# A gated projection stage split into three passes: seven block products for u and z, a DRAM round trip, and an output projection of two tiles per PSUM sum

## The reference

```python
def odd_mixer(h, sg_norm_g, w_in, w_spatial, b_spatial, w_out):
    p = jnp.einsum('bsd,de->bse', h, w_in)
    u, v, z = _split(p, ODD_SIZES)              # 2048 columns each
    u = jax.nn.gelu(u)
    v = rmsnorm(jax.nn.gelu(v), sg_norm_g)
    vg = v.reshape(B, nc, SG_CHUNK, SG_GROUPS, SG_GROUP_DIM)
    wm = w_spatial * causal
    vs = jnp.einsum('gts,bcsgd->bctgd', wm, vg) + b_spatial.T[None, None, :, :, None]
    y = u * vs.reshape(B, S, SG_WIDTH) * jax.nn.silu(z)
    return jnp.einsum('bse,ed->bsd', y, w_out)
```

## Time and profile before

| | us |
|---|---|
| median of 3 runs | 2878.29 (2877.9 to 2878.43) |
| the profiled execution: its own time | 2879.76 |
| its span, first to last instruction | 2878.0 |
| values stage and before | up to 2278.4 |
| gating stage, tiles 0 to 15 without the last pass | 2278.4 to 2828.2 |
| last pass, norm and store | 2828.2 to 2878.0 |

### The profile page before, as it was taken

The page is one execution under the profiler, slowest core; times in us unless marked ns, Lnnn a source line. Parts: engine busy times, 40 slices in busy tenths (PEclk is TensorE's granted clock), DMA queues, the critical chain, the costliest instruction groups (busy, mean ns, idle before and its releaser), DMA issues.

```text
span 2878.0 us, 38876 instructions
## 1 busy us (share of the span) xinstructions
PE 2753.0 (96%) x14218; PEld 2204.1 (77%) x14218; DVE 1497.4 (52%) x2252; ACT 889.8 (31%) x1500; POOL 1352.2 (47%) x792
## 2 busy tenths in 40 slices
PE   6999999999988999999998999999989999999997
PEld 2588888888776777777776888888688878888885
DVE  6665445455465555566556464546430045555555
ACT  3642322322253333334332323222431321111112
POOL 0587676776553322222221443433254465555564
PEclk9999999999999999999998999999999999999998
DMA  9211111111121110001001111211232311111123
GB/s 386 91 52 51 46 56 51 51 54 47 44 82 40 36 37 22 29 30 36 29 30 37 45 51 41 54 53 50 85 128 75 115 59 59 58 58 59 58 66 125
DMA packets 62904, 185.40 MB, mean 64 GB/s; under 512 B 17108, under 2 KB 23380, under 8 KB 60648
## 3 DMA queue, kind: packets, MB, share of 16 engines
q1 hardware_dynamic: 42016, 152.68, 15.9%
q10 hardware_dynamic: 20808, 31.61, 3.2%
HBM read 163.22 MB, written 21.05 MB: 64 GB/s over the span
## 4 chain that ended last, share of the span: by engine, by line
PE 85%; DVE 6%; issue 3%; ACT 3%; DMA 1%; POOL 1%; DVEq 0%; ACTq 0%; SPq 0%; POOLq 0%
PE ps L886 26%; PE ps L888 25%; PE ps L887 25%; PE ps L1297 2%; DVE acc L2570 1%; PE ps L954 1%; PE ps L1308 1%; DMA resid<-x_t 1%; PE ps L1060 1%; PE ps L1027 1%; PE ps L1654 1%; ACT sg_z L2346 1%; PE ps L1345 0%; PE ps L987 0%; DVE da_al L2787 0%
## 5 line engine op out<-in xcount | busy, mean ns | idle before, releaser
L637 POOL TENSOR_TENSOR slab_hi<-slab_raw,zero 128x1024 fp32r<-128x1024 f32 x165 | 328.7, 1992 | 1142.6 <-PE ps L888 997.0
L886 PE MATMUL ps<-h_hi,slab_hi 128*128 128x512 f32 x1936 | 771.1, 398 | 11.5 <-POOL h_lo L655 7.0
L887 PE MATMUL ps<-h_lo,slab_hi 128*128 128x512 f32 x1936 | 759.0, 392 | 0.0
L888 PE MATMUL ps<-h_hi,slab_lo 128*128 128x512 f32 x1936 | 758.2, 392 | 0.0
L886 PEld LDWEIGHTS ps<-h_hi,slab_hi 128*128 128x128 f32 x1936 | 365.8, 189 | 99.8 <-issue 15.4
L888 PEld LDWEIGHTS ps<-h_hi,slab_lo 128*128 128x128 f32 x1936 | 365.6, 189 | 79.2
L887 PEld LDWEIGHTS ps<-h_lo,slab_hi 128*128 128x128 f32 x1936 | 366.2, 189 | 72.4
L641 POOL TENSOR_TENSOR slab_lo<-slab_raw,slab_hi 128x1024 fp32r<-128x1024 f32 x165 | 413.0, 2503 | 14.6 <-DVE mean L2670 1.7
L2570 DVE TENSOR_TENSOR acc<-ps,acc 128x512 f32<-128x512 f32 x352 | 228.3, 686 | 24.7 <-PE ps L888 23.5
L2596 DVE SCALAR_TENSOR_TENSOR resid<-ps,mod,resid 128x512 f32<-128x512 f32 x320 | 224.6, 751 | 0.2
L702 POOL TENSOR_TENSOR slab_lo<-slab_raw,slab_hi 128x512 fp32r<-128x512 f32 x124 | 162.3, 1316 | 44.3 <-ACT slab_hi L1847 43.6
(11 more groups left out here) (371 smaller groups left out, 4977.3 us busy)
## 6 DMA issues: line engine op xcount, KB each, us to landing
slab_raw<-w_in SPq DMA_DIRECT2D x168, 512.0 KB, 3.6
mod_big<-mod_w SPq DMA_DIRECT2D x12, 2048.0 KB, 11.2
slab_raw<-w_c SPq DMA_DIRECT2D x43, 512.0 KB, 3.6
res_scr<-resid ACTq DMA_DIRECT2D x4, 2048.0 KB, 7.2
resid<-res_scr ACTq DMA_DIRECT2D x2, 4096.0 KB, 13.0
gv_scr<-sg_t ACTq DMA_DIRECT2D x4, 2048.0 KB, 7.0
slab_raw<-gv_scr SPq DMA_DIRECT2D x16, 512.0 KB, 3.4
resid<-x_t SPq DMA_DIRECT2D x2, 2048.0 KB, 16.3
```

What stands on the lines that cost most here:

```text
L637: pool.tensor_tensor(hi, raw[slot][:], zeros, ALU.add).then_inc(hi_done.sem, 1)
L886: pe.matmul(dst, w_h, r_h, start=first, stop=False, skip_group_check=True)
L887: pe.matmul(dst, w_h, r_l, start=False, stop=False, skip_group_check=True)
L888: return pe.matmul(dst, w_l, r_h, start=False, stop=last, skip_group_check=True)
```

## The change

The gating stage becomes three passes.

1. For each of the 16 tiles, u and z are made together as seven block products of 12 matmuls (84 instead of 96). ACT and DVE turn them into gelu(u) times silu(z) (`gu_` tiles), and the product is stored to DRAM (`uz_scr`). The input sums that the scheme needs are made by DVE during the values stage.
2. The spatial products no longer stand between u and z. Tiles 0 and 1 are done inside the last turn of pass 1, and the others inside pass 3.
3. The output projection takes two tiles at a time (`sg_pair`), both summed in PSUM before DVE adds 16 pieces per pair instead of 16 per tile. The stored `uz_scr` tile is read back and multiplied with the spatial result. The last two tiles keep their own last pass.

The scaled spatial weights are now made by ACT in eight pieces per group (one DVE instruction before). The high parts of the weight slabs move from POOL to ACT. POOL no longer clears `acc`. The last pass itself keeps its order.

```diff
+GATE_ORDER = (A11, S1, A12, S3, S4, S2, A22)
+GATE_LAST_ORDER = (A11, S3, S1, A12, S4, S2, A22)
+LAST_GATE = SG_TILES - 1
+SG_PAIRS = SG_TILES // 2 - 1
...
+            def load_gate(f, s):
+                sp.wait_ge(u_lo.sem, u_lo.at(f - 1, GATE_ORDER.index((A12, A22)[s])))
+                load_ring(f, s, w_in, 2 * f + (IN_SG + s), in_load[s])
+            def store_gate(f):
+                sp.wait_ge(u_mul.sem, u_mul.at(f))
+                sp.dma_start(uz_scr[bass.ds(f, 1)].rearrange("a p t -> p (a t)"), uz_out[:]).then_inc(uz_st.sem, 16)
...
+            def load_uz(d):
+                if d < 2:
+                    sp.wait_ge(u_mm.sem, u_mm.at(LAST_GATE, gate_product(LAST_GATE, S3)))
+                else:
+                    sp.wait_ge(e_yl.sem, e_yl.at(d - 2))
+                sp.wait_ge(uz_st.sem, uz_st.at(d))
+                sp.dma_start(uz[d % 2][:], uz_scr[d]).then_inc(uz_ld[d % 2].sem, 16)
...
+            def gate_sums(f):
+                for load in in_load:
+                    pool.wait_ge(load.sem, load.at(T_SG // 2 + f))
+                a21 = gate_source(S3)
+                pool.tensor_tensor(gu_s1[:], a21, gate_source(A22), ALU.add).then_inc(u_sum.sem, 1)
+                pool.wait_ge(u_sum.sem, u_sum.at(f, 0))
+                pool.tensor_tensor(a21, gate_source(A11), a21, ALU.subtract).then_inc(u_sum.sem, 1)
+                pool.tensor_tensor(gu_s2[:], gu_s1[:], gate_source(A11), ALU.subtract).then_inc(u_sum.sem, 1)
+                pool.wait_ge(u_sum.sem, u_sum.at(f, 2))
+                pool.tensor_tensor(gu_s4[:], gate_source(A12), gu_s2[:], ALU.subtract).then_inc(u_sum.sem, 1)
+            def gate_low(f, j):
+                pool.wait_ge(u_hi.sem, u_hi.at(f, GATE_ORDER.index(j)))
+                low, high = (gate_ring(tile, last, j).rearrange("p k f -> p (k f)") for tile, last in ((all_lo, u_lo6), (all_hi, u_hi6)))
+                pool.tensor_tensor(low, gate_source(j), high.bitcast(F32), ALU.subtract).then_inc(u_lo.sem, 1)
...
+            gate_sums(LAST_GATE)
+            for j in GATE_ORDER[:4]:
+                gate_low(LAST_GATE, j)
+            spatial_low(0)
+            for j in GATE_ORDER[4:]:
+                gate_low(LAST_GATE, j)
+            values_low(1)
+            for n in range(4):
+                slab_low(0, n)
+            y_low(0)
+            spatial_low(1)
+            y_low(1)
+            values_low(2)
...
+                last = q == SG_PAIRS - 1
+                if q > 0:
+                    slab_low(q, 2)
+                    slab_low(q, 3)
+                values_low(2 * q + 3)
+                y_low(2 * q + 2)
+                if last:
+                    split_c(TC_SG + SG_TILES)
+                else:
+                    slab_low(q + 1, 0)
+                    slab_low(q + 1, 1)
+                    values_low(2 * q + 4)
+                    spatial_low(q + 2)
+                y_low(2 * q + 3)
...
-            def sg_tile(d, e, g, first):
-                pe.wait_ge(e_u.sem, e_u.at(d - 1))
-                if first and e == 0:
-                    pe.wait_ge(v_g.sem, v_g.at(NC * (SV_SETS - 1) + 5))
-                project(T_SG + 2 * d, 0)
...
+            def gate_block(f, j):
+                pe.wait_ge(u_lo.sem, u_lo.at(f, GATE_ORDER.index(j)))
+                w_h, w_l = gate_ring(all_hi, u_hi6, j), gate_ring(all_lo, u_lo6, j)
+                r_h, r_l = GATE_INPUT[j]
+                for k in range(KT // 2):
+                    mm = three(FFN_BANK[j], w_h[:, k, :], w_l[:, k, :], r_h[:, k, :], r_l[:, k, :],
+                               k == 0 and j in FFN_OPENS, k == KT // 2 - 1)
+                mm.then_inc(u_mm.sem, 1)
...
+            def gate_ready(f, j):
+                if j == A11:
+                    pe.wait_ge(u_gate.sem, u_gate.at(f - 1, 0))
+                elif j == S1:
+                    pe.wait_ge(u_c.sem, u_c.at(f - 1, 0))
+                elif j == A12:
+                    pe.wait_ge(u_pc.sem, u_pc.at(f, 0))
+                elif j == S3:
+                    pe.wait_ge(u_c.sem, u_c.at(f - 1, 2))
+                elif j == S4:
+                    pe.wait_ge(u_pc.sem, u_pc.at(f, 1))
+                elif j == S2:
+                    pe.wait_ge(u_u.sem, u_u.at(f - 1))
+                else:
+                    pe.wait_ge(u_y.sem, u_y.at(f))
...
-            def sg_turn_out(g, e):
-                sg_tile(2 * g + e, e, g, False)
-                pe.wait_ge(e_v.sem, e_v.at(2 * g + e))
-                sg_out(2 * g + (e - 1), 1 - e, TC_SG + 4 * g + 2 * e)
...
+            gate_ready(0, A12)
+            gate_block(0, A12)
+            turned_ready(10)
+            gate_block(0, S3)
+            gate_ready(0, S4)
+            gate_block(0, S4)
+            pe.wait_ge(v_g.sem, v_g.at(NC * SV_SETS - 1))
+            turned_ready(11)
+            gate_block(0, S2)
+            gate_ready(0, A22)
+            turned_ready(15)
...
+            with pe.Fori(1, LAST_GATE) as f:
+                for j in GATE_ORDER:
+                    gate_ready(f, j)
+                    gate_block(f, j)
+            for j in GATE_LAST_ORDER:
+                if j == S3:
+                    sg_spatial(0)
+                if j == S4:
+                    sg_spatial(1)
+                gate_ready(LAST_GATE, j)
+                gate_block(LAST_GATE, j)
...
+            def sg_pair(q):
+                slabs = [(s, *sy[q % 2][s]) for s in range(2)]
+                for t in range(2 * KT):
+                    d, e = divmod(t, 2)
+                    if d % 4 == 0 and e == 0:
+                        pe.wait_ge(o_lo.sem, o_lo.at(q, d // 2 + 1))
+                    if t == 0:
+                        pe.wait_ge(e_yl.sem, e_yl.at(2 * q + 1))
+                    bank_free(q, t)
+                    for n, (s, r_h, r_l) in enumerate(slabs):
+                        mm = three(BANK[4 + t % 4], whi[s][:, d, :], wlo[s][:, d, :], r_h[:, half_of(e)], r_l[:, half_of(e)],
+                                   n == 0, n == 1)
+                    mm.then_inc(o_mm.sem, 1)
+                    if t in (1, KT - 1):
+                        sg_spatial(2 * q + (2 if t == 1 else 3))
+            for q in range(SG_PAIRS):
+                sg_pair(q)
...
+            def gate_high(f, j):
+                if j in RING_SUM_GATE:
+                    act.wait_ge(u_sum.sem, u_sum.at(f, RING_SUM_GATE[j]))
+                else:
+                    s = 1 if j == A22 else 0
+                    act.wait_ge(in_load[s].sem, in_load[s].at(T_SG // 2 + f))
+                act.activation(gate_ring(all_hi, u_hi6, j).rearrange("p k f -> p (k f)"), gate_source(j), ACT.Copy).then_inc(u_hi.sem, 1)
+            def gate_next(f, j):
+                act.wait_ge(u_mm.sem, u_mm.at(f - 1, gate_product(f - 1, j)))
+                gate_high(f, j)
...
+            def spatial_weights(g):
...
+                for c in range(NC):
+                    act.activation(wr[:, c, :], wsp[:, g, :], ACT.Identity, scale=stat[:, NC + c:NC + c + 1],
+                                   bias=zero[:, 0:1]).then_inc(w_s.sem, 1)
                 act.wait_ge(w_s.sem, w_s.at(g))
-                act.wait_ge(in_mm.sem, in_mm.at(T_SG + 4 * g - 1))
                 act.activation(wr_hi[:], wr[:], ACT.Copy).then_inc(w_h.sem, 1)
...
-            def sg_tile(d, e):
-                act.wait_ge(in_mm.sem, in_mm.at(T_SG + 2 * d))
-                act.wait_ge(e_y.sem, e_y.at(d - 1))
-                act.activation(sg_u[:], PS[0], ACT.Gelu_apprx_tanh).then_inc(e_u.sem, 1)
-                act.wait_ge(in_mm.sem, in_mm.at(T_SG + 2 * d + 1))
-                act.activation(sg_z[:], PS[1], ACT.Silu).then_inc(e_z.sem, 1)
-                act.wait_ge(e_y.sem, e_y.at(d))
-                act.activation(sy_hi[e][:], sg_v[:], ACT.Copy).then_inc(e_yh.sem, 1)
...
+            def gate_turn(f, first=False):
+                gate_copy_first(f, first)
+                gate_next(f + 1, A11)
+                gate_next(f + 1, S1)
+                gate_copy_fifth(f, first)
+                gelu_first(f, first)
+                for j in (A12, S3, S4, S2):
+                    gate_next(f + 1, j)
+                gelu_second(f)
+                gate_next(f + 1, A22)
+                silus(f)
+            for k in range(KT // 2):
+                act.wait_ge(tin_sum.sem, tin_sum.at(k))
+                act.wait_ge(c_mm.sem, c_mm.at(TC_SG - 1))
+                act.activation(h_hi[:, k, HALF:T], g4_raw[:, k, :], ACT.Copy).then_inc(tin_hi.sem, 1)
...
+            for j in (S4, S2):
+                gate_high(0, j)
+            act.wait_ge(v_st[1].sem, v_st[1].at(SV_SETS // 2 - 1))
+            gate_high(0, A22)
+            gate_turn(0, first=True)
...
+            with act.Fori(1, LAST_GATE) as f:
+                gate_turn(f)
+            spatial_weights(0)
...
+            def gate_sums(f):
+                dve.wait_ge(u_mm.sem, u_mm.at(f, gate_product(f, S2)))
```

(15 more changed lines are left out.)

455 lines of the change are left out of this document (338 added, 117 removed).

## The result

The changed kernel takes **2861.9 us** (median of 5 runs, 2859.7 to 2866.2) against 2878.3: ratio 0.9945, 95% interval 0.993 to 0.9959, so it is 16.4 us faster where 35.0 were forecast. The profiled execution is its fastest, 2859.7 us with a span of 2858.0.

A forecast was written before the change was run, and what follows sets the result against it. PE, by its number of matmuls, was taken as the bound. Work 493.0 plus waits 6, 13 and 5 gives 517.0 us against 549.8; with the last pass −35.0, so 2843.3 us, range 2832 to 2861.

The forecast's parts named there:

- Block products: Gating stage: seven products take 19.22 us per turn, 16 turns 307.5 against 351.4 before, −43.9 us.
- Spatial and output products: Gating stage: same pace, 28.6 and 156.9 us; the 6.4 and 6.5 us of old waits go.
- Turns 1 to 14: Gate turns: slab, ACT and POOL chains all fit under PE's 19.22 us, so 0 us extra.
- POOL's circle: POOL's repeating work per gate turn: load wait 3.8, four sums, seven low parts, 17.9 us, spare 1.3.
- The rival of a longer gate turn: Gate turns: hand-overs use up their spare and add 1.2 us a turn, 18 in all: 2861 us; 14%.
- POOL held off by DVE: Gate turns: DVE's passes over SBUF tiles slow POOL's pieces, 3.9 us per turn over PE, about 2901 us; 4%.
- Turn 0: First gate turn: PE waits 3.3 us after S1 and 2.3 before S4, a clock drop hidden; 6 us taken.
- Turn 15: Last gate turn: waits of 6.8, 1.6 and 2.4 us plus 2.1 for half clock, together 13 us.
- Pairs 0 to 5: Output pairs of 26.0 us: POOL's y part comes late, at least 26.8; 0.8 each, six times, 5 us.
- the pairs wait more: Output pairs: 2 us beyond the forecast wait in each of seven, 2857 us; 9%.
- Last pass: Final pass: its two waits of 1.1 us go, −2.2 us.

The follow-up runs named there:

- experiment 7: Changed kernel with the values' high part ahead of the spatial weights (2845.3 us), but output projections taking one tile at a time in PSUM: 2863.9 us.
- experiment 10: The kernel with ACT's copies of A11 and S1 moved earlier (2865.2 us), plus a DVE wait starting products after POOL's next A22 low part: 2858.7 us.
- experiment 5: Changed kernel with ACT's copy of A11 earlier in turn 0 and its copy of S1 ahead of the next turn's S1 part: 2865.2 us.

## Why the prediction was off

The direction and the mechanism of the gain were right, the size was not: 16.4 of 35.0 us came, and 2861.9 lies 0.9 above the range. Point by point, by the numbers of the prediction:

1. *Block products*: right. 19.27 us where 19.22 stood.
2. *Spatial and output products*: right. A pair's work is 26.1 us, the pace unchanged; experiment 7 shows that DVE's adds would cost 18.6 us more.
3. *Turns 1 to 14*: 0 extra, right in the sum. Its margin was not. I wrote that POOL's circle has a spare of 1.3 us; it is 0.9 (18.3 in experiment 10), and only while DVE's products fall in POOL's wait for the slabs. In experiment 5 they don't, the slabs come later too, and the circle is 19.9. The rival of a longer gate turn (14%) didn't happen. The rival "POOL held off by DVE", at 4%, named a part of this mechanism; it came not in the changed kernel but in the mended one, at 0.65 us a turn where the rival had 3.9.
4. *Turn 0*: right, 25.3 us for 25.2. The first wait is 2.98 for 3.3. Of the second nothing is seen, and that was forecast: half clock cost the products behind the first wait 3.0 us, and ACT's copy of S1 was done at 2293.85, 16.55 us after the values for 16.6, 0.4 before S4 began.
5. *Turn 15*: 2.8 short. Its three waits were sized well, 7.4, 2.6 and 1.4 us from matmul to matmul, less 0.23 each that is the pace, are 10.7 where 6.8 + 1.6 + 2.4 = 10.8 stood. The clock was not: 38.6 less 22.9 of work and 10.7 leaves 4.9 for 2.1. I costed one stretch of half clock, as long as the one in the earlier trace rows. After 7 us of waiting the spatial product and two blocks behind it, 7.3 us of work, took 10.7, from 2582.33 until ACT could copy S1 (row below). The other 1.6 us are a second stretch, behind the wait of 2.20.

```profile
2593.01 0.60 ACT L2654 ACTIVATE gu_p<-ps 128x512 f32<-128x512 f32 x1 [12.14 <-PE ps L1048]
```

6. *Pairs 0 to 5*: **the step that failed**, 5 us forecast, 18.4 more than 6 × 26.0 measured. I had the right chain (y stands last on POOL) and took 0.8 a pair for its overhang. It is 2.1: in pair 0 ACT starts its weights at 15.5 us and not at 14.9, its chain takes 5.2 and not 4.7, as a 128-column piece is 0.40 (3.20 for eight) and not 0.33, and POOL's first part 2.98 and not 2.4, as DVE's product falls beside it. Three small terms, all rounded the kind way, on a chain whose slack was already below zero. And the consequence I left out altogether: behind such a wait the clock may halve, 1.6 us each, here at three of six heads. Waits 12.4 and clock 4.7 make 17.1 of the 17.5 above 6 × 26.15. The rival "the pairs wait more" (9%) is what happened.
7. *Last pass*: right, 2858.0 − 2811.38 = 46.6 us where 49.8 were before, so −3.2 for −2.2. The values ended 1.1 us sooner too (2277.3 for 2278.4), which no item had. Both were luck on my side: the stage is 17.1 us over, the span 15.0.

The last 3.6 us are not the trace's: I took the median 0.3 above the profiled span, and the profiled execution was the fastest of five. Part of the runs' spread lies ahead of the stage; what it comes from stays open.

Of the drain of 1380 ns that the Trainium skill ("ScalarE: Activation LUTs", "What ACT_TABLE_LOAD costs") adds to a table load the trace after shows nothing: the load starts 0.03 us after the activation before it has ended, and the activation behind it 1.29 us after the load, so 1.28 was the right term.

```profile
2572.59 0.63 ACT L2546 ACTIVATE gu_hi<-slab_raw 128x512 fp32r<-128x512 f32 x1 [0.72 <-PE ps L1048]
2573.25 1.28 ACT L2671 ACT_TABLE_LOAD   x1
2574.54 0.63 ACT L2671 ACTIVATE gu_u<-gu_u 128x512 f32<-128x512 f32 x1
```
